# Rounding a third unit of expert values in each group of four, with its low parts made on VectorE

## The reference

```
ue  = take(expert_u, picks)                      # 16384 x 2048, float32
act = gelu(einsum('nhkd,nd->nhk', ue, x)) * gates
out = einsum('nhk,nhkd->nd', act, take(expert_v, picks))
```

## Time and profile before

| what | value |
|---|---|
| median of 3 runs | 2312.44 us (2311.9 to 2318.38) |
| the profiled execution's own time | 2314.51 us |
| its span from first to last instruction | 2312.7 us, 1.8 us less than its time |
| PE busy, DVE busy, POOL busy | 97%, 64%, 40% of the span |
| stage V (L961's first start to L967's last) | 1614 to 2290 us |

### The profile page before, as it was taken

How to read it: one execution, slowest core, us unless ns; L and a number is a source line. 1 busy time by engine, 2 the same in 40 slices (tenths; PEclk the granted TensorE clock), 3 DMA queues, 4 the chain that set the end, 5 groups by cost and what they waited for, 6 DMA issues and landing times.

```text
span 2312.7 us, 42095 instructions
## 1 busy us (share of the span) xinstructions
PE 2242.3 (97%) x14906; PEld 2078.6 (90%) x14906; DVE 1483.0 (64%) x2267; ACT 1033.5 (45%) x1961; POOL 925.6 (40%) x686
## 2 busy tenths in 40 slices
PE   8999999999999999999999999999999999999997
PEld 8888787988888888999999999999999989899997
DVE  5558888548567565765654599996456656666512
ACT  5447554444554554555555444444333333233333
POOL 0000300200000000546766766665666767767654
PEclk9999999999999999999999999999999999999999
DMA  6665555136666657568888888886888888888885
GB/s 212 189 192 157 153 164 163 49 92 182 192 195 203 205 164 229 197 213 332 331 318 308 325 311 318 320 319 218 303 314 312 322 321 308 298 309 330 298 257 178
DMA packets 206399, 566.64 MB, mean 245 GB/s; under 512 B 15717, under 2 KB 83815, under 8 KB 188647
## 3 DMA queue, kind: packets, MB, share of 16 engines
q1 hardware_dynamic: 187719, 430.23, 56.0%
q0 software_dynamic: 18592, 135.27, 15.6%
HBM read 559.09 MB, written 5.24 MB: 244 GB/s over the span
## 4 chain that ended last, share of the span: by engine, by line
PE 74%; DMA 13%; POOL 5%; DVE 3%; issue 2%; ACT 2%; SPq 1%; ACTq 0%; DVEq 0%
PE PS L902 13%; DMA raw<-in_peer_v 12%; PE PS L544 10%; PE PS L894 7%; PE PS L967 6%; PE PS L587 5%; PE PS L589 5%; PE PS L588 5%; PE PS L546 5%; PE PS L897 4%; POOL w_lo L1480 4%; PE PS L537 3%; PE PS L961 3%; PE PS L964 2%; PE PS L910 2%
## 5 line engine op out<-in xcount | busy, mean ns | idle before, releaser
L1480 POOL TENSOR_TENSOR w_lo<-raw,w_hi 128x512 fp32r<-128x512 f32 x512 | 691.5, 1373 | 436.5 <-ACT w_hi L1303 435.2
L1303 ACT ACTIVATE w_hi<-raw 128x512 fp32r<-128x512 f32 x512 | 294.2, 622 | 523.3 <-DMA raw<-in_peer_v 432.6
L1534 DVE TENSOR_TENSOR w_lo<-raw,w_hi 128x512 fp32r<-128x512 f32 x552 | 374.0, 691 | 235.6 <-ACT w_hi L1027 234.1
L1027 ACT ACTIVATE w_hi<-raw 128x512 fp32r<-128x512 f32 x552 | 345.5, 632 | 359.7 <-PE PS L589 180.9
L544 PE MATMUL PS<-act_both,w_hi 128*128 128x512 f32 x1056 | 373.7, 400 | 6.7 <-DVE w_lo L1534 6.0
L967 PE MATMUL PS<-onehot,raw 128*128 128x192 f32 x2016 | 353.9, 329 | 6.8 <-DMA raw<-in_peer_v 5.5
L902 PE MATMUL PS<-big,raw 128*128 128x192 f32 x2048 | 356.8, 327 | 1.9 <-DMA raw<-in_peer_u_t 1.9
L967 PEld LDWEIGHTS PS<-onehot,raw 128*128 128x128 f32 x2016 | 327.0, 191 | 8.4 <-DMA raw<-in_peer_v 5.7
L902 PEld LDWEIGHTS PS<-big,raw 128*128 128x128 f32 x2048 | 330.0, 190 | 2.2 <-DMA raw<-in_peer_u_t 2.2
L2188 DVE TENSOR_TENSOR act_both<-big,act_both 128x192 fp32r<-128x192 f32 x128 | 119.7, 935 | 302.5 <-ACT act_both L1392 302.5
L546 PE MATMUL PS<-act_both,w_lo 128*128 128x256 f32 x990 | 278.7, 282 | 0.0
(11 more groups left out here) (278 smaller groups left out, 2985.8 us busy)
## 6 DMA issues: line engine op xcount, KB each, us to landing
raw<-in_peer_u_t SPq DMA_DIRECT2D x256, 512.0 KB, 4.6
raw<-in_peer_v SPq DMA_DIRECT2D x256, 512.0 KB, 6.2
raw<-in_w_in SPq DMA_DIRECT2D x180, 512.0 KB, 3.7
raw<-in_w_out SPq DMA_DIRECT2D x32, 512.0 KB, 4.8
raw<-in_peer_w_q SPq DMA_DIRECT2D x32, 512.0 KB, 3.4
raw<-in_w_ret_branch SPq DMA_DIRECT2D x16, 512.0 KB, 3.8
raw<-in_w_rwkv_branch SPq DMA_DIRECT2D x16, 512.0 KB, 3.8
big<-in_x SPq DMA_DIRECT2D x2, 1024.0 KB, 6.0
```

Source lines behind the costliest of these rows:

```text
L1027: act.activation(w_hi[:, slot % 2, hh * 512:(hh + 1) * 512], raw[:, slot, hh * 512:(hh + 1) * 512], ACT.Copy).then_inc(S["unit_hi"], 1)
L1480: pool.tensor_tensor(w_lo[:, k // 2, cols], raw[:, k, cols], w_hi[:, k // 2, cols].bitcast(f32), ALU.subtract).then_inc(S["p_split"], 1)
L1534: dve.tensor_tensor(w_lo[:, slot % 2, cols], raw[:, slot, cols], w_hi[:, slot % 2, cols].bitcast(f32), ALU.subtract).then_inc(S[done], 1)
```

## The change

In stage V the unit k = 3 becomes a rounded one too (`V_ROUNDED` is (0, 2, 3)); stage U is as it was. Its low parts of the weights are made on DVE (`d_split`), where those of k = 0 and 2 stay on POOL (`p_split`), and its low part of the activations is a third subtraction on DVE. `act2` gets a third place, and `v32` is left with one. Since three rounded units now share two places of `w_hi` and `w_lo`, a unit takes the place (3 * par + index) % 2, where par is the parity of the iteration: the loops go over two iterations at a time. `LAG` says how many units back the one lies that used the place before: 2 for k = 0, 3 for k = 2 and k = 3. The load of k = 3 waits for DVE's low parts instead of PE's multiplication.

```
-U_ROUNDED, V_ROUNDED = (0, 2), (0, 2)
+U_ROUNDED, V_ROUNDED = (0, 2), (0, 2, 3)
+U_SPLIT = {"p_split": (0, 2), "d_split": ()}
+V_SPLIT = {"p_split": (0, 2), "d_split": (3,)}
+LAG = {0: 2, 2: 3, 3: 3}
...
-        v32 = onehot2[:, 0:2 * DT].rearrange("p (s n) -> p s n", s=2)
+        v32 = onehot2[:, 0:DT]
...
         def split_done(stage, it, k, halves):
-            return S["p_split"], rounded(stage, it, k, halves)
+            name = "p_split" if k in (U_SPLIT if stage == "u" else V_SPLIT)["p_split"] else "d_split"
+            return S[name], counted(U_SPLIT[name], V_SPLIT[name], stage, it, k, halves)
+
+        def w_slot(stage, par, k):
+
+            return k // 2 if stage == "u" else (len(V_ROUNDED) * par + V_ROUNDED.index(k)) % 2
...
-            def vm(h, it, k, first=False):
+            def vm(h, it, par, k, first=False):
                 if k in V_ROUNDED:
-                    pe.wait_ge(S["act2_split"], it * 2 + (h * (BLOCKS // 2) + k // 2 + 1))
+                    pe.wait_ge(S["act2_split"], it * 3 + (h * (3 * BLOCKS // 4) + V_ROUNDED.index(k) + 1))
+                    at, acts = w_slot("v", par, k), act2[:, V_ROUNDED.index(k)]
...
-            def round_unit(stage, m, it, k):
+            def round_unit(stage, m, it, k, par=0, again=False):
...
-                        act.wait_ge(S["half_used"], m * 8 + (2 * k - 7 + hh))
+                        act.wait_ge(S["half_used"], m * 8 + (2 * k + hh + 1 - 2 * (4 if stage == "u" else LAG[k])))
                     cols = slice(hh * 512, (hh + 1) * 512)
-                    act.activation(w_hi[:, k // 2, cols], raw[:, k, cols], ACT.Copy).then_inc(S["unit_hi"], 1)
+                    act.activation(w_hi[:, w_slot(stage, par, k), cols], raw[:, k, cols], ACT.Copy).then_inc(S["unit_hi"], 1)
...
-                if g >= UPAIRS and k in V_ROUNDED:
-                    low_parts("v", g - UPAIRS, k)
+                if g >= UPAIRS and k in V_SPLIT["p_split"]:
+                    low_parts("v", g - UPAIRS, g % 2, k)
...
+                    if k in V_SPLIT["d_split"]:
+                        for hh in range(2):
+                            dve.wait_ge(*hi_done("v", g - UPAIRS, k, hh + 1))
+                            at, cols = w_slot("v", g % 2, k), slice(hh * 512, (hh + 1) * 512)
+                            dve.tensor_tensor(w_lo[:, at, cols], raw[:, k, cols], w_hi[:, at, cols].bitcast(f32), ALU.subtract).then_inc(S["d_split"], 1)
```

More of the change, by code:

```diff
@@ L1006, in _, with v_blocks @@
             for h in range(2):
-                def v_blocks(it, first=False, final=False):
+                def v_blocks(it, par, first=False, final=False):
                     for k in range(2 if final else 4):
-                        vm(h, it, k, first and k == 0)
+                        vm(h, it, par, k, first and k == 0)
                     if final:
                         last_units(h)
-                v_blocks(0, first=True)
-                with pe.Fori(1, BLOCKS // 4 - 1) as it:
-                    v_blocks(it)
-                v_blocks(BLOCKS // 4 - 1, final=True)
+                v_blocks(0, 0, first=True)
+                v_blocks(1, 1)
+                with pe.Fori(1, BLOCKS // 8 - 1) as i:
+                    for par in range(2):
+                        v_blocks(i * 2 + par, par)
+                v_blocks(BLOCKS // 4 - 2, 0)
+                v_blocks(BLOCKS // 4 - 1, 1, final=True)
         @block.scalar
@@ L1391, in v_hi @@
                     row = rowof(4 * it + k if isinstance(it, int) else it * 4 + k)
-                    act.activation(act2[:, k // 2, 0, :] if k in V_ROUNDED else v32[:, k // 2, :], row, ACT.Copy).then_inc(S["act2_hi"], 1)
+                    act.activation(act2[:, V_ROUNDED.index(k), 0, :] if k in V_ROUNDED else v32, row, ACT.Copy).then_inc(S["act2_hi"], 1)
                     if k in V_ROUNDED:
-                        round_unit("v", it + (V0 + h * BLOCKS) // 4, it, k)
+                        round_unit("v", it + (V0 + h * BLOCKS) // 4, it, k, par, start and h == 1)
                     if start and h == 0 and k == 0:
@@ L1402, in v_hi, with v_his, body @@
                         odd_out(4 * k + 3)
-            run_loop(act, 0, EARLY // 4, lambda it: v_hi(0, it))
+            def v_his(h):
+                def body(i):
+                    for par in range(2):
+                        v_hi(h, i * 2 + par, par)
+                return body
+            run_loop(act, 0, EARLY // 8, v_his(0))
             act.wait_ge(S["late"], BLOCKS - EARLY)
-            with act.Fori(EARLY // 4, BLOCKS // 4) as it:
-                v_hi(0, it)
-            run_loop(act, 0, BLOCKS // 4, lambda it: v_hi(1, it))
+            run_loop(act, EARLY // 8, BLOCKS // 8 - EARLY // 8 + EARLY // 8, v_his(0), 0)
+            run_loop(act, 0, BLOCKS // 8, v_his(1))
             def square_last(tt, q):
@@ L1479, in low_parts @@
                     cols = slice(hh * 512, (hh + 1) * 512)
-                    pool.tensor_tensor(w_lo[:, k // 2, cols], raw[:, k, cols], w_hi[:, k // 2, cols].bitcast(f32),
+                    at = w_slot(stage, par, k)
+                    pool.tensor_tensor(w_lo[:, at, cols], raw[:, k, cols], w_hi[:, at, cols].bitcast(f32),
                                        ALU.subtract).then_inc(S["p_split"], 1)
```

51 lines of the change are left out of this document (26 added, 25 removed).

## The result

The changed kernel is slower. Its median is 2353.51 us (4 runs, 2344.55 to 2364.27), that of the kernel before in the same comparison 2314.07 us (4 runs, 2311.9 to 2318.38): a ratio of 1.0169, with a 95% interval of 1.0137 to 1.0201, so 39 us more.

The account below looks back on a forecast made before the run. PE, busy 97% of the span, was taken as the bound, with 48 us of waits in stage V. PE's -19 us and the waits' -8 us made -27 us, so a median of 2285 us; range 2258 to 2326.

Parts of the forecast that it names:

- the slower rival: Stage V: DVE and POOL become the bound once DVE reaches 10.63 us an iteration; 2332 us (2319 to 2345), chance 0.18.
- PE's term: PE in stage V: 64 plain units become rounded, each 0.30 us shorter, -19 us (-15 to -22).
- The step that failed: DVE and POOL in stage V: DVE's load of 8.8 to 10.8 us an iteration, middle 9.8, fits below 10.2.
- the term of -8 us for the waits: PE's waits in stage V, 48 us now: 20 us could go, some 12 come back; -8 us (-40 to +50).
- the bound of +50: Upper end for PE's waits: 52 iterations delayed by a sparse step's 1 us, +50 us at the most.
- its sign of being wrong: Stage V: the prediction is wrong if PE's waits move by more than 20 us either way.
- SP's queue: Loads: one of two holds an iteration goes, 64 turns waiting for PE; nothing up to 39.7 us of PE's waits gained.
- Places: Two places of w_hi: k = 0's rounding, one unit (2.3 us) ahead, fits with 1 us to spare; +50 us at most.
- The loads: Rival: loads are the bound and stay it, the iteration staying at 10.4 us or more; around 2308 us, chance 0.18.
- The queue was everything: Rival: loads arrive before they are needed, PE runs at 9.5 us plus 0.15; 2262 us, chance 0.20.

Follow-up runs that it names:

- act_k0_first: Changed kernel, with the next k = 0's activations rounded on ACT and split on DVE ahead of k = 3's weights; 2351.87 us, ratio 1.0169 to the kernel before.
- three_places: Changed kernel with a third place for w_hi and w_lo, so each unit may be rounded four units ahead; 2354.57 us, ratio 1.0191 to the kernel before.
- acts_ahead: Changed kernel with activations rounded and subtracted an iteration ahead, into six places of act2; 2329.27 us, ratio 1.0068 to the kernel before.
- acts_ahead_three_places: Changed kernel with activations made an iteration ahead and a third place for w_hi and w_lo; 2326.66 us, ratio 1.0037 to the kernel before.
- short_sparse_after: Changed kernel with sparse steps adding 8 columns in place of 1024, the rest left out; 2327.63 us, ratio 1.0076 to the kernel before.
- weights3_on_pool: Changed kernel with the low parts of k = 3's weights made on POOL too; 2378.03 us, ratio 1.0259 to the kernel before.
- dve_all_low: Changed kernel with all low parts of stage V's weights made on DVE, POOL left with its gathers; 2296.41 us, ratio 0.9885 to the kernel before.
- before_dve_all_low: Kernel before, with two rounded units, and both units' low parts in stage V made on DVE; 2306.39 us, ratio 0.9935 to the kernel before.
- pool_only_writes: Changed kernel, POOL in stage V writing zeros to w_lo instead of subtracting for k = 0 and 2; 2301.80 us, ratio 0.9959 to the kernel before.

## Why the prediction was wrong, point by point

The measured 2353.5 us lies above the range, and above that of the slower rival too (2319 to 2345).

*PE's term was right.* 64 x 0.30 = -19 us was forecast, with an iteration of 9.5 us where nothing is late; the steps without a wait sum to 9.47, against 9.79, so -20.

*The step that failed is the one on DVE and POOL*: "The middle, 9.8, is below 10.2; the cover is DVE's present idling (3.6 us each iteration)", and with it the term of -8 us for the waits, which measured +55 us, beyond the bound of +50 and by far more than the 20 us that the prediction named as its sign of being wrong. (The 3.6 us also don't come out of the rows: 10.63 - 6.44 = 4.2.) The prices were inside their bounds: 1.07 us for a new subtraction, 0.90 for the one of the activations (0.94 forecast); DVE's load, 8.85 us, was at the lowest end of 8.8 to 10.8. What was wrong is the measure. DVE's load was held against the length of an iteration, as if it could be done anywhere in it. But DVE works in order, and the low part for k = 0 stands behind two low parts and a sparse step that can be held by POOL. ACT's rounding for it was done a median of 3.7 us before PE was free for k = 0, and one held instruction takes 2.3 to 3.9 us. DVE's idle time lies elsewhere: 172 us of it in front of L2206, waiting for ACT.

*The slower rival had the right mechanism and the wrong condition.* It was to decide "from where DVE reaches today's 10.63", with 1.6 us for each new subtraction. It decided at 8.85 us and 1.07. A sum that would have warned is that of what the two engines do with two inputs, at undisturbed durations, since while one runs the other mostly stands. With 1.26 us for a half on POOL, 0.35 and 0.69 for DVE's subtractions, 1.28 for a sparse step and 2.5 of those in an iteration, gathers left out:

| kernel | POOL + DVE, us an iteration | measured iteration, 1700 to 2200 us |
|---|---|---|
| before | 4 x 1.26 + 2 x 0.35 + 2.5 x 1.28 = 8.9 | 10.63 |
| changed | 8.9 + 0.35 + 2 x 0.69 = 10.7 | 11.44 |
| act_k0_first, three_places | 10.7 | 11.24, 11.49 |
| acts_ahead, acts_ahead_three_places | 10.7 | 10.91, 10.89 |
| short_sparse_after (0.21 for a sparse step) | 8.0 | 10.71 |
| weights3_on_pool | 6 x 1.26 + 3 x 0.35 + 3.2 = 11.8 | 11.80 |
| dve_all_low | 6 x 0.69 + 3 x 0.35 + 3.2 = 8.4 | 10.27 |
| before_dve_all_low | 4 x 0.69 + 2 x 0.35 + 3.2 = 6.7 | 10.33 |

Measured iterations are 32000 us over PE's instructions in that stretch. PE needs 9.5 us with three rounded units. Before, the shared sum was below PE's 9.8; the change took it above PE, to 10.7. One kernel runs just at its sum and two 0.2 above it, but three with the same 10.7 run 0.5 to 0.8 above it, and short_sparse_after, whose sum is below PE's 9.5, takes 10.71. Nor is the sum a strict bound: in weights3_on_pool it comes to 504 us for the stretch of 500, while by the starts and lengths in the trace an instruction of the one kind or the other ran for 459 of them and neither for 41, so they overlap a little and the agreement at 11.80 is in part chance. That the sum limits an iteration is therefore not shown; that taking POOL out of it removes the loss is shown by dve_all_low.

The Trainium skill ("SBUF — State Buffer", Who interferes with whom) has the rule: a VectorE instruction with two SBUF inputs excludes a GpSimd instruction that reads SBUF, but not one that only writes it. The traces agree with both halves of it: beside POOL's subtractions DVE's instructions took 1.80, 1.07 and 0.90 us at the mean, beside POOL's writes in pool_only_writes 1.28, 0.69 and 0.36. The prediction cited the rule, and then held the middle of DVE's bounds against the iteration, without asking when each result is due.

*SP's queue.* The count was right and the gain was not there. In the changed kernel's stage V, SP's waits (against the earlier trace rows) were:

```profile
SPq L502 <- PE PS L975: 285.1, 63, 9.0
SPq L502 <- POOL w_lo L1497: 200.6, 93, 5.8
SPq L502 <- DVE w_lo L2211: 41.5, 50, 3.2
```

There are 63 waits for PE in place of 125, but the three sum to 527 us, against 495 for the two before: much of the hold moved to POOL and DVE, whose low parts free the buffers.

*Places.* That k = 0 fits with a unit of lead held against ACT and POOL: three_places changed nothing. ACT did wait for the place (92.6 us), which cost nothing that three_places could give back.

*The loads.* They were not the bound. Over 1640 to 2200 us of the changed kernel, to be held against the earlier trace rows:

```profile
raw<-in_peer_v SPq DMA_DIRECT2D x197, 512.0 KB, 7.1
```

There were fewer loads (197 against 211) at 298 GB/s against 310, and they took longer to land (7.1 against 6.3 us) at a DMA share of 0.84 against 0.87. In dve_all_low the same stretch moved 321 GB/s, above the 310 from which the prediction had worked out that a rival would stay slow.

*The queue was everything* (2262 us) is out as well: with DVE and POOL apart, 2284 to 2299 was reached, with 36 to 45 us of waits left. (Its sum was off too: 0.15 us in 64 iterations leaves 10 of the 48 us, so -38 and not -31.)

## What to carry to other kernels

When two engines hold each other up, each engine's own busy share shows room that isn't there: its waiting counts as busy, and its idle time may lie where nothing needs it. Add up what both do that excludes the other, at undisturbed durations, and take it as a warning when the sum comes near the time that the engine they feed needs; here it was no exact bound. Then ask of each result when it is due and what can stand before it. To take work from the engine that is slower can beat balancing: POOL needs 1.26 us for a half and DVE 0.69, and giving DVE all of them shortened this kernel, though DVE looked the fuller of the two. And a stall that moves along the same engine's queue when its order is changed (act_k0_first) says that another order alone won't remove it; a longer lead (acts_ahead) gave back a part, and moving POOL's subtractions away gave back more than all of it.

## What was unexpected of the hardware

DVE came off worse in the mutual holds: in the changed kernel POOL's half took 1.45 us at the mean in place of 1.26 at the least, DVE's 192 columns 0.90 in place of 0.35. One hold can last through several of POOL's instructions. A sparse step of 1.28 us clear took 3.92, from the end of a gather's issue through both halves of a pair, and the low part behind it, 0.34 us long, was late for PE by 2.36 us (timeline of the changed kernel, DVE, POOL and PE):

```profile
1806.54 3.92 DVE L2127 SCALAR_TENSOR_TENSOR big<-inv,big 128x1024 f32<-128x1024 f32 x1
...
1810.38 0.34 DVE L2206 TENSOR_TENSOR act_both<-big,act_both 128x192 fp32r<-128x192 f32 x1
```

```profile
1805.62 1.22 POOL L1510 DMA_INDIRECT inv<-in_peer_v,big  x1 [0.15 <-issue]
1806.86 2.50 POOL L1497 TENSOR_TENSOR w_lo<-raw,w_hi 128x512 fp32r<-128x512 f32 x2
```

```profile
1804.69 0.88 PE L969 MATMUL PS<-act_both,w_hi 128*128 128x384 f32 x4
...
1810.86 1.58 PE L969 MATMUL PS<-act_both,w_hi 128*128 128x384 f32 x4 [2.36 <-DVE act_both L2206]
```

The step starts 0.3 us before POOL's pair and ends after it. The same page of the Trainium skill ("SBUF — State Buffer", SBUF: two separate sides) says that whichever of two such instructions starts first gets the shared pair of ports for its whole length. The trace of the changed kernel's stage V agrees where POOL was doing nothing: of 40 DVE instructions with two inputs that started then, and met a subtraction of POOL's within their undisturbed length, 37 were not held. It doesn't where a gather was being issued: of 21 that started then and met a subtraction behind it, 14 were held for more than 1 us. The gather by itself holds nothing: in dve_all_low 74 DVE instructions started during one, and all kept their undisturbed length. Why the first of two loses there stays open.

After this wait PE was slower for some microseconds. Stretches ahead of it, behind it and later, with PE's clock as the third number from the end:

```profile
1804.00:1808.00 4.00, 3.84 (x25) 3.58 (x26) 4.00 (x4) 2.58 (x7) 3.83 (x4) 1.00 0.70 211
1810.80:1814.30 3.50, 3.44 (x12) 3.45 (x13) 3.50 (x3) 0.44 (x2) 3.34 (x3) 0.52 0.95 392
1816.00:1820.00 4.00, 4.00 (x28) 4.00 (x27) 2.56 (x4) 1.28 (x4) 0.55 (x1) 1.00 0.91 330
```

The granted clock was at 0.52 in the 3.5 us behind the wait, about its lower level of 1.2 GHz, and four multiplications took 1.58 us in place of 0.88. So a stall can cost PE more than its own time, though not each time: five of the eight stalls of 2.4 us at k = 0 led into such a stretch. In all, stage V of the changed kernel had the lower clock (0.50) in eight stretches, 31 us together, the kernel before in three with 10 us, dve_all_low in none. At half the clock that is, as an estimate from these lengths, up to 10 of the 33 us that stage V grew by. Each of the eight stretches began in or just behind waits of PE.
